# First layer's experts: the turnings of token rows and of context rows issued as two blocks of eight

## What is computed

```python
def ec_ffn(h, router_w, w_gate, w_up, w_down):
    n_tok, d = h.shape[1], h.shape[2]
    cap = EC_CAPACITY_FACTOR * n_tok // N_EXPERTS      # 128 of the latents, 32 of the context
    aff = jax.nn.softmax((h @ router_w).astype(jnp.float32), axis=-1)
    top_aff, idx = lax.top_k(jnp.swapaxes(aff, 1, 2), cap)
    xg = jax.vmap(lambda hb, ib: hb[ib])(h, idx)
    hid = silu(xg @ w_gate) * (xg @ w_up)              # per expert, 1024 -> 512
    y = (hid @ w_down) * top_aff[..., None]            # per expert, 512 -> 1024
    return zeros.at[idx].add(y)
```

## Time and profile before

| what | value |
|---|---|
| three runs | 4461.4, 4451.52, 4456.78 us |
| median | 4456.78 us |
| span of the profiled execution | 4445.8 us |
| mean granted TensorE clock over the span | 0.940 |
| TensorE matmul busy | 4031.7 us (91%) |
| VectorE, ScalarE, GpSimd busy | 2167.2, 1301.5, 506.4 us |
| first layer's expert stage, first turning to last down product | 1081.7 to 1576.5 us of the span |

### The profile page before, as it was taken

One profiled execution on the slowest core, in us unless ns is written; L12 is line 12 of the kernel. 1 busy time (PEld: TensorE's weight loads), 2 busy tenths in 40 slices (PEclk: granted clock), 3 DMA queues, 4 the chain that ended last, 5 costly groups with the idle time before them and its releaser, 6 DMA issues. The chain is left out here.

```text
span 4445.8 us, 51677 instructions
## 1 busy us (share of the span) xinstructions
PE 4031.7 (91%) x20694; PEld 3142.7 (71%) x20694; DVE 2167.2 (49%) x3353; ACT 1301.5 (29%) x2259; POOL 506.4 (11%) x597
## 2 busy tenths in 40 slices
PE   7989999897999979898988799799976999998997
PEld 5878655664777769785656699677744778887875
DVE  3577655423111155676553433475565365554444
ACT  3234533222111132344333233311344211112232
POOL 1000111102212210002111111200102100000011
PEclk8999999997999989998999899899887999999999
DMA  6000000337766641000012799312001211112111
GB/s 247 33 20 1 16 1 1 139 155 314 260 249 236 210 173 39 15 1 16 1 67 107 273 337 346 106 48 86 21 1 53 76 43 48 48 48 82 50 57 57
DMA packets 73878, 453.30 MB, mean 102 GB/s; under 512 B 8000, under 2 KB 12624, under 8 KB 57680
## 3 DMA queue, kind: packets, MB, share of 16 engines
q1 hardware_dynamic: 56960, 389.73, 23.2%
q0 software_dynamic: 13088, 47.19, 3.9%
q10 hardware_dynamic: 3632, 13.63, 0.8%
HBM read 394.95 MB, written 55.57 MB: 101 GB/s over the span
## 5 line engine op out<-in xcount | busy, mean ns | idle before, releaser
L2290 PEld LDWEIGHTS psum<-words,words 128*128 128x128 f32 x4096 | 514.6, 192 | 10.4 <-issue 9.1
L2290 PE MATMUL psum<-words,words 128*128 128x160 f32 (+1 forms) x4096 | 515.9, 289 | 1.4 <-DVE words L392 0.9
L675 PE MATMUL psum<-words,words 128*128 128x512 f32 x1104 | 440.6, 399 | 32.3 <-DVE words L715 27.9
L676 PE MATMUL psum<-words,words 128*128 128x512 f32 x1104 | 441.6, 400 | 0.0
L677 PE MATMUL psum<-words,words 128*128 128x512 f32 x1104 | 436.8, 396 | 0.0
L1605 PE MATMUL psum<-words,words 128*128 128x428 f32 (+1 forms) x720 | 253.2, 352 | 29.4 <-DVE words L1698 29.4
L675 PEld LDWEIGHTS psum<-words,words 128*128 128x128 f32 x1104 | 210.9, 191 | 86.3 <-DVE words L715 29.4
L1317 PE MATMUL psum<-words 128*128 128x512 f32 (+1 forms) x504 | 255.1, 588 | 0.0
L1606 PE MATMUL psum<-words,words 128*128 128x428 f32 (+1 forms) x720 | 249.9, 347 | 0.0
L1607 PE MATMUL psum<-words,words 128*128 128x428 f32 (+1 forms) x720 | 249.1, 346 | 0.0
L677 PEld LDWEIGHTS psum<-words,words 128*128 128x128 f32 x1104 | 209.8, 190 | 48.4
(11 more groups left out here) (436 smaller groups left out, 7986.8 us busy)
## 6 DMA issues: line engine op xcount, KB each, us to landing
words<-in_w_gate SPq DMA_DIRECT2D x32, 2048.0 KB, 8.0
words<-in_w_up SPq DMA_DIRECT2D x32, 2048.0 KB, 12.5
words<-in_w_down SPq DMA_DIRECT2D x32, 2048.0 KB, 12.9
words<-in_ada_w SPq DMA_DIRECT2D x24, 2048.0 KB, 14.6
words<-in_w_in SPq DMA_DIRECT2D x55, 512.0 KB, 3.4
words<-in_w_up SPq DMA_DIRECT2D x44, 512.0 KB, 3.4
words<-in_w_down SPq DMA_DIRECT2D x44, 256.0 KB, 2.6
words<-in_x SPq DMA_DIRECT2D x2, 5120.0 KB, 22.5
```

Of the source, the lines that this page charges most:

```text
L675: pe.matmul(out, hi[:, j, w], S.parts[0](kt, t0, nt), start=(kt == 0), stop=False)
L676: pe.matmul(out, hi[:, j, w], S.parts[1](kt, t0, nt), start=False, stop=False)
L2290: mm = pe.matmul(k.bank[m % 2][:, u * W:(u + 1) * W], ring[:, side[j], w0:w0 + P], xgT[:, j, kt, 0:W], start=(kt == 0), stop=(kt == KD - 1))
```

## The change

In the first layer, `transposes` now issues the eight token turnings first, over the three banks, and then the eight context turnings, over the same three banks. The waits for the banks stay in the first loop. `t_full` rises, as before, once for each bank, now at the bank's last context turning. For the second layer (`with_ctx` false) the second loop is empty and the order stays as it was. Shapes, places, number of instructions, copies and all other engines' programs are the same.

```diff
@@ -2268,9 +2268,13 @@
                     for kt in range(k0, k0 + kn):
                         c0 = (kt - k0) * W
                         mm = pe.transpose(k.bank[2 + g][:, c0:c0 + P], xg[:, j, kt * P:(kt + 1) * P], k.ident[:, :])
-                        if with_ctx:
-                            mm = pe.transpose(k.bank[2 + g][:, c0 + P:c0 + W], xc[0:CAP_C, j, kt * P:(kt + 1) * P],
-                                              k.ident[0:CAP_C, 0:CAP_C])
+                    if not with_ctx:
+                        mm.then_inc(t_full, 1)
+                for g, (k0, kn) in enumerate(groups if with_ctx else []):
+                    for kt in range(k0, k0 + kn):
+                        c0 = (kt - k0) * W
+                        mm = pe.transpose(k.bank[2 + g][:, c0 + P:c0 + W], xc[0:CAP_C, j, kt * P:(kt + 1) * P],
+                                          k.ident[0:CAP_C, 0:CAP_C])
                     mm.then_inc(t_full, 1)
```

## The result

The changed kernel takes 4404.7 us (median of 4, 4399.6 to 4412.5) against 4454.2 us for the kernel before (median of 4) in the same comparison: a ratio of 0.9887, 95% interval 0.9873 to 0.9901, so 49 us less (44 to 57). Forecast was 4421.0 with a range of 4411 to 4437. The direction and the mechanism were right; the gain was undersized, and the low end of the range lay 6 us above the measured time.

A forecast was written before the change was run, and what follows sets the result against it. TensorE was taken to bound the stage. Savings of 20.1 us (15 groups), 14.7 (clock falls) and 1.0 (expert 0) summed to 35.8, taken from 4456.8: 4421.0 us, range 4411 to 4437.

The forecast's parts named there:

- Bound: In the experts' stage TensorE is busy 493.10 of 494.76 us, so what it saves is saved from the span.
- Token turnings, 0.117 us apart: Eight token turnings in a steady group: 7 distances of 0.117 us, read from the second layer's run, make 0.82 us.
- Context turnings, taken at 0.117 us: Eight context turnings in a steady group: 7 distances of 0.117 us make 0.82 us, bounded by 0.11 and 0.17 each.
- The change to 32 rows, 0.26 us: In each steady group, one change from token to context turnings costs 0.26 us, then 0.17 to the down product.
- The clock, 14.7 us: After the groups, nine of 15 windows had clock falls; all were expected to go, saving 14.7 us, bounds 0 and 14.7.
- Expert 0, 1.0 us within 0 to 2.4: Expert 0's group at clock 0.50 shrinks from 5.1 to some 3.2 us; its gate product gives one back: 1.0 saved.
- The distance of 11.0 us between span and median: Runs' median lies 11.0 us above the profiled span of 4445.8 us; taken as fixed to reach 4456.8 us.
- The falls stayed: Rival for the gaps after the groups: clock falls stay, only distances shrink, saving 21.1 us, 4435.7 us; 16%.
- the context turnings drew closer: Rival in the groups denied this: context turnings stay 0.17 us apart, group 2.44 us, saving 30.3, 4426.5 us; 10%.
- the order did matter: Rival in the groups denied this: waits have another cause than row count, nothing changes, 4456.8 us; 3%.
- the slower case: Rival in the groups: context turnings 0.37 us each, group 4.04 us, six more falls, 4475.9 us; 2%.
- Covers: Edits costed at nothing: bank copies, silu and multiply, gather and weight DMAs around the group stay covered.

The follow-up runs named there:

- run 2: Changed kernel with context turnings as plain products padded to 128 active rows (96 of them zeros): group 2.67 us, stage 459.0 us.
- run 9: Changed kernel with context turnings as plain products with the identity (two passes each), 32 active rows: group 2.86 us, stage 463.4 us.
- Run 4: Changed kernel with each context turning issued five times into the same place: group 3.57 us, seven of 15 windows with a clock fall.
- run 7: Changed kernel with each token turning issued three times into the same place: group 3.32 us, all 15 windows at clock 1.00.
- run 8: Changed kernel plus window attention scores put in blocks by active rows: 4344.7 us, ratio 0.9772 to the kernel before.
- run 12: The changed kernel once more, against the kernel before in five rounds: 4404.0 us against 4453.7, ratio 0.9891.
- run 11: Changed kernel with the eight context turnings (32 rows) moved between token turnings 0 and 1: group 1.73 us, stage 444.1 us, whole 4405.0 us.
- run 1: Kernel before, its order kept, with context turnings as plain products padded to 128 active rows: group 2.35 us, stage 453.7 us.
- run 6: Kernel before, its order kept, with context turnings as plain products of 32 active rows: group 4.69 us, stage 520.2 us.

## Why the prediction was right or wrong

- **Bound.** Right: TensorE bounds the stage, and no wait took the place of the one removed. The medians fell by 49 us with 45.1 gained in the stage, so nothing of it was lost on the way that the scatter lets one see.
- **Token turnings, 0.117 us apart.** Right: 0.11, so 0.77 us and not 0.82. The 0.117 was a mean that held one slower distance (0.165) at the start of the second layer's run.
- **Context turnings, taken at 0.117 us.** This is the step that failed. I took the distance "since 128 weight columns is what both runs share" and named 0.11 as the bound near below. It measured 0.065, outside my bounds. The rows behind it, 128x2 and 16x512, are plain fp32 products. The passes of such a product with 32 columns through stand 0.11 us apart with 128 active rows and with 32 (runs 2 and 9); a transpose of 32 or 64 rows and columns does not share that. The term was 0.82 and is 0.46: 0.36 x 15 = 5.4 us. As lower bound I should have gone beneath the plain products, since no row showed a short transpose in a run.
- **The change to 32 rows, 0.26 us, and back, 0.17.** They were 0.20 and 0.15. The 0.26 was read behind a token turning that had itself waited (length 0.33); in a run the length is 0.27. With the token term this makes 0.13 x 15 = 2.0 us more.
- **The clock, 14.7 us.** Right in cause and size: all nine falls are gone. Run 4 has falls with only two changes of rows a group; run 7 has none in a dense group nearly as long, and neither has the long dense run in combine. So it is the long sparse stretch that brings them. Why nine of 15 like groups had one and six had none stays open.
- **Expert 0, 1.0 us within 0 to 2.4.** It gave 3.0, above its bound. Its turnings and the wait behind them fell from 5.8 to 3.6 us, and the gate product, instead of paying one back, got 0.7 us shorter (19.03 at clock 0.92, against 19.76 at 0.88): the clock rose 3.2 us after that product's start, against 4.7 before (3.4 and 3.5 in runs 8 and 12). Part of this can be luck: in run 11, whose first group is nearly as short (3.7 us), the rise came 5.9 us after that start and the product took 20.4.
- **Sum.** 35.8 forecast, 45.1 in the stage: 9.3 us short, of which 7.4 is the distances and 2.0 expert 0. The kernel before also measured 2.6 us less in the paired runs, and the rest of the miss of 16.3 us, some 4, is what run 12 leaves open. The low end allowed for scatter, for expert 0 at its bound and for later falls; a term of the group itself that saves more than forecast had no room in it.
- **The distance of 11.0 us between span and median**, taken as fixed. It isn't: a run with both numbers has 4406.4 and 4404.6, 1.8 apart. The profiled execution before was simply a quick one, of some 4447.6 us by that distance. It did no harm here, since the saving was taken off the median.
- **Rivals.** The falls stayed nowhere; the context turnings drew closer than forecast; the order did matter; the slower case didn't come. The case that did come, context turnings closer than 0.11 us, was not among them.
- **Covers.** The silu and multiply still end inside the group, though only 0.7 us ahead of the down product now (1158.07 against 1158.79); the gather and the weights were never waited for in the loop.

## What to carry to other kernels

Where TensorE goes back and forth between full and small numbers of active rows (128 against 64 or 32 here), look at the distance between starts rather than at busy time: each change cost 0.13 us for the turnings and 0.18 for the attention's scores, and TensorE looked 91% busy throughout. Put products with the same active rows together, as far as the accumulation and the banks allow. A long stretch of such sparse, waiting work costs a second time when the clock falls behind it (1.6 us for each fall here), which the profile books on the products that follow.

## What the runs showed of the hardware that was not expected

- A plain fp32 product shows as two passes. In a run of such products with 32 columns through they stand 0.11 us apart, with 32 rows and with 128 (runs 2 and 9). A transpose is one pass; in a run they stand 0.06 us apart with 32 or 64 rows and columns, and 0.11 with 128.
- What makes TensorE wait is the change of the active rows: with the same instructions in the same order, a pair takes 0.28 us with 128 rows throughout and 0.59 with 128 and 32 in turn (runs 1 and 6).
- Issuing every token turning three times costs 1.74 us a group (3.32 against 1.58) and not one clock fall; issuing every context turning five times costs 2.0 us and brings seven falls.
